# A two-block decoder on one core: where three waits, one norm scale and eleven pieces of an output projection stand in the written order

## The reference, cut to what matters

```python
# first block, layer i: adaLN, attention, adaLN, gated convolution FFN
h = rmsnorm(x, norm_mix[i]) * (1.0 + sc1) + sh1
x = x + g1 * attention_i(h, hc)            # i=0: difference attention, i=1: neighbourhood attention
h2 = rmsnorm(x, norm_ffn[i]) * (1.0 + sc2) + sh2
x = x + g2 * conv_ffn(h2, ...)
...
return rmsnorm(x, norm_out)                # = the second block's input

# second block, layer l
h = rmsnorm_2(x, norm_g[l])
proj = h @ w_in[l]                          # split into nsa q/kv, gates, pool, conv, fox q/k/v, merges
blocks = k[:, idx] + pos_emb                # nsa_compress: windows of 32 tokens, stride 16
flat = blocks.reshape(B, nc, NSA_CMP_LEN * hd)
return jax.nn.silu(flat @ w1 + b1) @ w2 + b2
...
return x + acc @ w_out
```

## Time and profile before

| | us |
|---|---|
| median of 3 runs | 1644.51 (1643.88 to 1645.31) |
| profiled execution, its own time | 1647.73 |
| its span (first to last instruction) | 1645.4 |
| PE busy | 1601.1 (97%) |
| DVE, ACT, POOL busy | 922.3, 766.5, 542.8 (56%, 47%, 33%) |
| mean granted TensorE clock | 0.991 |

### The profile page before, as it was taken

How to read it: one execution, slowest core, us unless ns; L and a number is a source line. 1 busy time by engine, 2 the same in 40 slices (tenths; PEclk the granted TensorE clock), 3 DMA queues, 4 the chain that set the end, 5 groups by cost and what they waited for, 6 DMA issues and landing times.

```text
span 1645.4 us, 24642 instructions
## 1 busy us (share of the span) xinstructions
PE 1601.1 (97%) x9872; PEld 1348.4 (82%) x9872; DVE 922.3 (56%) x1477; ACT 766.5 (47%) x1408; POOL 542.8 (33%) x358
## 2 busy tenths in 40 slices
PE   7999998999999999999999999999999999999998
PEld 4777556777777888879767899999999999999987
DVE  3344475455423654342265888658476567768545
ACT  4323485354312443253375655445454555554553
POOL 2214144222211222221273111026224567423554
PEclk9999999999999999999999999999899999999999
DMA  9164510433155212364313654545434544533551
GB/s 396 65 245 163 214 43 27 174 133 146 69 198 214 94 70 75 127 210 155 120 35 132 257 179 167 172 173 181 144 129 154 179 154 174 199 129 129 179 197 59
DMA packets 52976, 249.26 MB, mean 151 GB/s; under 512 B 20608, under 2 KB 21760, under 8 KB 26368
## 3 DMA queue, kind: packets, MB, share of 16 engines
q1 hardware_dynamic: 44400, 244.42, 41.1%
q10 hardware_dynamic: 8464, 3.28, 0.8%
HBM read 246.63 MB, written 1.05 MB: 151 GB/s over the span
## 4 chain that ended last, share of the span: by engine, by line
PE 90%; DVE 6%; ACT 2%; issue 1%; DMA 1%; POOL 0%; POOLq 0%; DVEq 0%; ACTq 0%
PE psq L545 14%; PE psq L547 14%; PE psq L546 14%; PE psq L921 7%; PE ps L545 6%; PE ps L547 6%; PE ps L546 6%; PE psq L922 4%; PE ps L921 3%; PE ps L559 2%; PE ps L922 1%; DVE WL L527 1%; PE psq L1324 1%; PE ps L1352 1%; PE psq L2215 1%
## 5 line engine op out<-in xcount | busy, mean ns | idle before, releaser
L527 POOL TENSOR_TENSOR WL<-RAW,WH 128x1024 fp32r<-128x1024 f32 (+2 forms) x116 | 299.6, 2585 | 551.8 <-ACT WH L517 540.7
L527 DVE TENSOR_TENSOR WL<-RAW,WH 128x1024 fp32r<-128x1024 f32 (+3 forms) x264 | 323.8, 1251 | 272.5 <-ACT WH L517 272.3
L517 ACT ACTIVATE WH<-RAW 128x1024 fp32r<-128x1024 f32 (+2 forms) x380 | 361.0, 1001 | 166.8 <-DMA RAW<-wstream 116.4
L545 PE MATMUL psq<-NHL,WH 128*128 128x256 f32 (+1 forms) x1264 | 413.4, 327 | 5.3 <-DVE WL L527 2.5
L547 PE MATMUL psq<-NHL,WL 128*128 128x256 f32 (+1 forms) x1264 | 407.5, 322 | 0.0
L546 PE MATMUL psq<-NHL,WH 128*128 128x256 f32 (+1 forms) x1264 | 407.4, 322 | 0.0
L545 PEld LDWEIGHTS psq<-NHL,WH 128*128 128x128 f32 x1264 | 242.2, 192 | 34.6 <-issue 8.7
L547 PEld LDWEIGHTS psq<-NHL,WL 128*128 128x128 f32 x1264 | 242.1, 192 | 18.1
L546 PEld LDWEIGHTS psq<-NHL,WH 128*128 128x128 f32 x1264 | 242.1, 192 | 16.9
L921 PE MATMUL psq<-NHL,WH 128*128 128x512 f32 x416 | 148.6, 400 | 0.0
L545 PE MATMUL ps<-NHL,WH 128*128 128x256 f32 (+1 forms) x368 | 122.1, 332 | 0.0
(11 more groups left out here) (378 smaller groups left out, 2861.3 us busy)
## 6 DMA issues: line engine op xcount, KB each, us to landing
RAW<-wstream SPq DMA_DIRECT2D x196, 1024.0 KB, 4.9
RAW<-wstream SPq DMA_DIRECT2D x32, 704.0 KB, 4.0
K<-first SPq DMA_DIRECT2D x4, 1024.0 KB, 15.6
X<-xin SPq DMA_DIRECT2D x2, 1024.0 KB, 6.0
V<-first SPq DMA_DIRECT2D x2, 1024.0 KB, 19.0
Q<-first SPq DMA_DIRECT2D x2, 1024.0 KB, 25.0
BR<-rpb ACTq DMA_DIRECT2D x8, 256.0 KB, 7.7
BR<-rpb SPq DMA_DIRECT2D x8, 256.0 KB, 8.6
```

The source lines that it names most:

```text
L517: e.activation(WH[:, u % 3, a:z], RAW[:, v % 3, a:z], ACT.Copy).then_inc(w_hi, 1)
L527: e.tensor_tensor(WL[:, u % 3, a:z], RAW[:, v % 3, a:z], WH[:, u % 3, a:z].bitcast(F32), ALU.subtract).then_inc(w_lo_p if pool else w_lo_v, 1)
L545: e.matmul(o, lh, rh, start=start, stop=False)
```

## The change

Five groups of edits, all of order and waiting, and one added copy:

1. In `act_qkv`, layer 0, unit 7: the split of the unit three ahead moves behind the reads of unit 7's banks and the ada row.
2. In `pe_diff`: the six pieces k = 0 to 5 of ("wo", 0, 0) stand in steps 32 to 37 (before five, in 33 to 37), and five pieces of ("wo", 0, 1) in steps 38 to 42. `pe_wo` begins at k = 6 and k = 5.
3. In `pe_wo`, layer 1: the piece (6, 0) of ada stands before the sums 4 and 5 and no longer behind them.
4. Ada turn 4 and its DVE step come two steps later in the second FFN chunk.
5. In the second block: DVE keeps a copy of NB's second half (`RS_KEPT`), the compression waits for this copy (`rs_kept`) and no longer for X, `dve_out_gain` reads the copy and moves behind the first causal maximum; and in both layers the lo half of "kf" moves between the flats of kind 0 and kind 1.

```diff
@@ act_qkv
             for u, i in enumerate(QKV_ORDER[l]):
                 key = ("qkv", l, i)
-                split_hi(e, ahead(key))
+                if (l, u) != (0, 7):
+                    split_hi(e, ahead(key))
...
                 if l == 0 and i == 7:
                     act_ada_row(e, 1)
+                    split_hi(e, ahead(key))
@@ pe_diff
-                if 33 <= n < 38:
-                    if n == 33:
+                if 32 <= n < 38:
+                    if n == 32:
                         e.wait_ge(att_exp, 62)
-                    pe_abreast(e, ("wo", 0, 0), [bank[0], bank[1]], (n - 33,), pe_wait_heads)
+                    pe_abreast(e, ("wo", 0, 0), [bank[0], bank[1]], (n - 32,), pe_wait_heads)
+                if 38 <= n < 43:
+                    if n == 38:
+                        e.wait_ge(att_exp, 64)
+                    pe_abreast(e, ("wo", 0, 1), [bank[2], bank[3]], (n - 38,), pe_wait_heads)
@@ pe_wo
                     if i == 0:
-                        pe_abreast(e, ("wo", l, i), [bank[b], bank[b + 1]], range(5, DT), wait_x)
+                        pe_abreast(e, ("wo", l, i), [bank[b], bank[b + 1]], range(6, DT), wait_x)
+                    elif i == 1:
+                        pe_abreast(e, ("wo", l, i), [bank[b], bank[b + 1]], range(5, DT), lambda e, k: None)
...
+                if (l, i) == (1, 3):
+                    pe_ada(e, 6, 0)
                 for m in range(2 * i - 2, 2 * i):
                     if m >= 0:
                         pe_sums(e, n, m)
-            pe_ada(e, 6 if l else 3, 0)
+            if l == 0:
+                pe_ada(e, 3, 0)
@@ second FFN chunk (PE; DVE likewise)
-                    if l == 0 and c == 1 and jj == 1:
+                    if l == 0 and c == 1 and jj == 3:
                         pe_ada_turn(e, 4)
@@ dve_out_gain
-            rs = NB[:, 256:512] if n == 5 else NB[:, 0:256]
-            e.wait_ge(rs_bc, NORM_AT[n] + 1)
+            e.wait_ge(rs_kept, 1)
             e.wait_ge(x_res, x_ready(n, DT - 1))
...
-                                       in1=rs, op0=ALU.mult, op1=ALU.mult).then_inc(x_res, 1)
+                                       in1=RS_KEPT, op0=ALU.mult, op1=ALU.mult).then_inc(x_res, 1)
@@ dve_raw_norm, at its end
+            if l == 0:
+                e.tensor_copy(RS_KEPT, NB[:, 256:512]).then_inc(rs_kept, 1)
@@ dve_head
                     e.tensor_tensor(dst, src, SMALL[ps, at:at + 16].unsqueeze(2).to_broadcast([64, 16, 15]),
                                     ALU.add).then_inc(flat, 1)
+                if kind == 0:
+                    lo_prep(e, l, "vn", False)
             e.memset(FHL[:, 1024:1152].bitcast(U32), 0).then_inc(flat_lo, 1)
-            lo_prep(e, l, "vn", False)
...
             lo_prep(e, l, "kf", False)
-            if l == 0:
-                dve_out_gain(e, 5, "nout")
@@ pe_compress_up
-            e.wait_ge(x_res, X_BASE[6 + l])
+            e.wait_ge(rs_kept, 1)
@@ dve_layer
             dve_causal_max(e, l, 0)
+            if l == 0:
+                dve_out_gain(e, 5, "nout")
             dve_gates(e, l, 2)
```

More of the change, by code:

```diff
@@ L481, in bass_two_block_decoder @@
             sem(n) for n in ("sb_copy", "flat", "flat_hi", "flat_lo", "cm_zero"))
-        raw_hi, raw_lo, raw_copy, raw_rs, x_gain = (sem(n) for n in ("raw_hi", "raw_lo", "raw_copy", "raw_rs", "x_gain"))
+        raw_hi, raw_lo, raw_copy, raw_rs, rs_kept, x_gain = (
+            sem(n) for n in ("raw_hi", "raw_lo", "raw_copy", "raw_rs", "rs_kept", "x_gain"))
         nrot_v, nrot_c, fx_v, fx_a, fx_tr, gs_a, gs_v = (
@@ L1681, in dve_ffn @@
                                                in1=a3[:, :, 0:255], op0=ALU.mult, op1=ALU.add).then_inc(up_tap, 1)
-                    if l == 0 and jj == (9 if c == 0 else 1):
+                    if l == 0 and jj == (9 if c == 0 else 3):
                         dve_ada(e, 3 + c)
@@ L1813, in pe_raw_head @@
             tiles("kn", (0, 1), range(DT)).then_inc(gemm, 1)
-        RS_ROW = TMP[:, 5, 0:256]
+        RS_ROW, RS_KEPT = TMP[:, 5, 0:256], TMP[:, 5, 256:512]
         def dve_raw_out(e, l, name):
```

## The result

A *stop* is idle time of PE between two of its instructions; a *slow stretch* is time in which the granted clock is at its lower level, 0.50.

A forecast was written before the change was run, and what follows sets the result against it. PE was taken to bound the kernel, busy 1601.1 of 1645.4 us. Terms 4.0 + 4.7 + 1.0 + 0 + 2.6 + 7.9 + 0 = 20.2, off the median 1644.51, gave 1624.3; 8-in-10 range 1620 to 1636.5.

The forecast's parts named there:

- layer 0 of edit 5: Layer 0's compression starts earlier, gaining 2.6 us, and its slow stretch goes, gaining 7.9; bounds together 0 to 10.7.
- the 1.7 of clock: Key unit and first attention: removing each place's stop also removes the slow stretch behind it, 1.7 us each.
- Compression, layer 1: Second block, layer 1: the removed 1.26 us wait for "kf" reappears before the compression as 1.9 idle; gain 0.
- a sign of being wrong: Layer 1's compression: any slow stretch behind the stop there would show the forecast wrong.
- the first rival: Layer 1's compression: the stop grows to about 1.9 us and the clock falls, costing 7.9; 1632.2 us, chance 0.24.
- the 3.2 known beforehand: Whole kernel: the profiled execution before lay 3.22 us above its runs' median, subtracted to forecast the new median.
- take the place of the gains: Layer 0's compression: DVE's lo half goes behind POOL's operation, so 2.6 and 7.9 stay out; 1634.8 us, chance 0.12.
- DVE did not win in layer 1: Layer 1's compression: rival that DVE is 0.3 us faster and goes first, gaining another 1.9; 1622.4 us, chance 0.08.
- That the slow stretches do not come from the stops: All three slow places: stretches come regardless, only stops pay, gain 8.9 us; 1635.6 us, chance 0.07.
- The slower side: From layer 1's compression into gates and causal attention: low clock lasts 47 us, making the kernel slower; chance 0.02.

The follow-up runs named there:

- the first trace of before: The unchanged kernel before the change, its originally profiled execution: 1647.73 us, span 1645.4; median of its 4 runs 1644.32.
- the two further ones: The kernel before, unchanged, run twice more for traces: 1645.02 and 1642.38 us (8 runs each); profiled executions 1642.0 and 1652.7.
- the changed kernel's second set: The changed kernel run again with no edit, 12 runs: 1634.54 us, ratio 0.9958 to the kernel before.
- the later sets: The unchanged kernel before, run beside the follow-up kernels; its median was 1639.6, 1641.1 and 1644.2 us in different sets of runs.
- the third experiment: Changed kernel plus 18 identity transpositions on PE in the stop before layer 1's compression: 1630.80 us, ratio 0.9930 to the kernel before.
- the second experiment: Changed kernel with DVE's lo half of the compression's first weights ahead of k's rotation in both layers: 1623.86 us, ratio 0.9890 to before.

## Why the prediction was wrong

**Right, to half a microsecond.** Edit 1 (4.29 for 4.0), edit 2 (4.71 for 4.7, with the 0.6 and 0.2 that stay), edit 3 (1.08 for 1.0), edit 4 (0), and layer 0 of edit 5 (10.59 for 10.5). Of the 10.59, 7.95 is clock, and that it agrees is in part luck: the first trace of before had the slow stretch, and one of the two further ones had not. In layer 0 the order came out as forecast, DVE ahead by 0.43 where half a microsecond was put. Taking an edit out again gave the same sizes for edits 1 and 2 (4.33 and 4.76), and for edit 3 a stretch that agrees. That the 1.7 of clock went with the stops of edits 1 and 2 held in every trace that has them.

**The step that failed** is "Compression, layer 1": "the 1.26 only turns up in the next stop: 0 gained". The first half held: the compression starts when it would have, and the idle turned up, 2.39 where 1.9 was put. But 0 was the wrong price: the slow stretch behind the stop, which the prediction named as a sign of being wrong, came and cost 7.95. With the first rival's mechanism, at its price (7.9 forecast), the sum is 12.3. It was given a chance of 0.24; the runs show the slow stretch behind a 2.4 us stop there in all three traces that have it and, by the times, in eleven of the twelve executions of the changed kernel's second set. What I used against it, that 1.81 us of idle at 903.32 had no slow stretch behind it, was one draw, an outcome that differs from execution to execution: both further traces of before have one behind the same stop, and so has the kernel without edits 3 and 4 (1.80, and 0.57 behind it).

**What was left of the difference.** The two profiled executions are 12.9 apart (1647.73 and 1634.80), the medians 8.6, because the profiled execution of before lies 3.4 over its runs and that of after 0.9 under. I carried the 3.2 known beforehand as an offset that both kernels share. That step failed too: with layer 1 at its right price the forecast gain would still have been 3.7 over the measured one.

The 67 executions of before in the later sets run from 1635.4 to 1653.3, 28 of them under 1641. Their mean clocks part them without overlap: 31 with 0.993 to 0.997 take 1635.4 to 1642.2, 36 with 0.985 to 0.991 take 1642.9 to 1653.3. Of the three traced ones, that without a long slow stretch has 0.995, that with one 0.991, and that with two 0.985. So, by this sign, layer 0's 7.9 is paid by about half of the executions of before at most, and one trace does not price it. It does not explain the 3.4, though: the four timed runs, 1643.9 to 1645.3, lie with the 36 by their times. What made the profiled execution longer than these stays open; starts differ by up to 4.9 between traces.

**The other rivals.** POOL did not take the place of the gains in the first weights; in the second weights DVE's operation was held up, in the trace of the third experiment. DVE did not win in layer 1. That the slow stretches do not come from the stops does not hold in layer 1, where filling the stop kept the clock up in the trace, and five of eight executions have a mean clock of 0.994 or more, where the changed kernel has one of twelve. The Trainium skill, "TensorE: Matmul & The Clock Gate", section "HAM oscillation — how this bites in real kernels", names longer gaps than these as the cause; the falls behind 2.39, 1.80 and 1.51 do not agree with it, and here they decide. The slower side did not come: no slow stretch lasted over 20 us.

The version that the second experiment found beats both: 0.9890 of before, where the change reached 0.9948 and 0.9958.

## What to carry to other kernels

Removing only the first of two waits can gain nothing, and can lose: here two short stops became one longer, and on PE that longer one was followed by some 17 us at half clock, a loss of 8. Follow a freed instruction to its next release before counting it, and either remove that too (here by moving one DVE operation ahead of another) or leave both. And a slow stretch seen in one trace is a draw: price it by how often it appears over several.

## What the runs showed that was not expected

- The clock's fall behind the same stop of 1.5 us came in three traces and not in a fourth, of the same program or one that differs only later; with a stop of 0.66 it came once. Stops of 2.3 to 2.5 us at the key unit, in the attention and in layer 1 were followed by one all 13 times, in eight traces, while the wait for a weight transfer near 705, 2.3 to 2.9 us in four traces, went with one in one of them.
- The length of the stop alone does not decide. The stop of 1.64 at the end of the table's third stretch (1.47 in one trace) and one of 1.45 at 430.10 in the first trace stand in all twelve traces, and none was followed by a fall.
- The clock can also fall with a short stop or none. At the sums behind layer 1's output projection it fell in four of the seven traces with a stop of 0.82 (0.60 from 896 to 900 in the changed kernel), and in three of the five with 1.81. In the third experiment it fell at the sums behind layer 0's output projection, where PE's row shows no idle time above 0.06 from 296 on:

```profile
306.00:314.00 8.00, 7.48 (x48) 4.04 (x47) 1.80 (x6) 1.04 (x3) 1.02 (x1) 0.79 0.89 312
```

- In the compression it stays down for some 17 us in five cases (a loss of 8) and some 14 in the two of the second further trace of before (a loss of 6.3 to 6.4); at the key unit and in the attention for 3.4 (a loss of 1.7).
- DVE and POOL do not meet at semaphores only. Of two lo halves begun within 0.05 us of each other, either can be the one held up; DVE's then takes 2.2 us longer (3.40 for 1.22), at the cost of whoever waits for it.
